# k and v of each DeltaNet head turned by VectorE in 32x32 blocks and a bounce through memory, in place of ten TensorE transposes

## What is computed

```python
qkv = silu(short_conv(qkv, conv_w)); q, k = l2norm(q), l2norm(k)
tinv = inverse(strict_lower(kb @ k.T * decay) + eye)   # u and w come from it
kd = k * exp(gc[-1] - gc)[:, None]
def step(s, xs):                                       # scan over chunks of tokens
    v_new = u_i - w_i @ s
    o_i = qg_i @ s + a_i @ v_new
    s = s * gl_i + kd_i.T @ v_new
```

## Time and profile before

| | before |
|---|---|
| median of 3 runs | 1302.97 us (1302.94 to 1303.77) |
| the profiled execution: time | 1302.37 us |
| the profiled execution: span | 1300.6 us |
| TensorE busy | 1284.3 us (99% of the span) |
| VectorE busy | 962.6 us (74%) |
| ScalarE busy | 701.2 us (54%) |
| mean memory traffic | 111 GB/s |

### The profile page before, as it was taken

How to read it: one execution, slowest core, us unless ns; L and a number is a source line. 1 busy time by engine, 2 the same in 40 slices (tenths; PEclk the granted TensorE clock), 3 DMA queues, 4 the chain that set the end, 5 groups by cost and what they waited for, 6 DMA issues and landing times.

```text
span 1300.6 us, 26090 instructions
## 1 busy us (share of the span) xinstructions
PE 1284.3 (99%) x9814; PEld 1212.4 (93%) x9814; DVE 962.6 (74%) x2396; ACT 701.2 (54%) x1578; POOL 172.8 (13%) x161
## 2 busy tenths in 40 slices
PE   7999999999999999999999999999999999999998
PEld 6898999999999999999988889999999999999998
DVE  6677867667686867767456666668999698987995
ACT  5564746465564746465366664347564355634643
POOL 1002020202001020200302320000103300041022
PEclk9999999999999999999999999999999999999999
DMA  9743543434243334325335216431323323233313
GB/s 313 242 131 96 166 122 100 118 94 118 55 142 90 116 103 120 89 72 153 115 113 169 77 51 207 124 82 33 98 67 97 98 70 93 66 100 96 83 57 106
DMA packets 207715, 144.51 MB, mean 111 GB/s; under 512 B 9455, under 2 KB 197015, under 8 KB 207463
## 3 DMA queue, kind: packets, MB, share of 16 engines
q1 hardware_dynamic: 207303, 142.72, 37.4%
q10 hardware_dynamic: 288, 0.13, 0.0%
HBM read 126.67 MB, written 17.99 MB: 111 GB/s over the span
## 4 chain that ended last, share of the span: by engine, by line
PE 92%; DVE 3%; SPq 2%; ACT 1%; issue 1%; DMA 1%; DVEq 0%; ACTq 0%
PE ps L1311 32%; PE ps L1957 25%; PE ps L1700 7%; PE ps L1615 3%; PE ps L1841 2%; PE ps L1937 2%; PE ps L1553 2%; PE ps L1622 2%; SPq L931 2%; PE ps L1439 1%; PE ps L1634 1%; PE ps L1809 1%; PE ps L1285 1%; PE ps L1795 1%; PE ps L1916 1%; PE ps L1693 1%
## 5 line engine op out<-in xcount | busy, mean ns | idle before, releaser
L1311 PE MATMUL ps<-hT_r,WAH_r 128*128 128x320 f32 x624 | 154.9, 329 | 0.5
L1311 PE MATMUL ps<-xT_r,WAH_r 128*128 128x320 f32 x624 | 142.0, 309 | 0.0
L1957 PE MATMUL ps<-d_part_r,W_r 128*128 128x320 f32 x660 | 136.7, 310 | 1.1 <-DVE xT L3388 0.7
L1311 PE MATMUL ps<-hT_r,W_r 128*128 128x320 f32 x588 | 132.6, 308 | 0.0
L1311 PEld LDWEIGHTS ps<-hT_r,WAH_r 128*128 128x128 f32 x624 | 100.3, 189 | 10.8 <-issue 9.8
L1957 PEld LDWEIGHTS ps<-d_part_r,W_r 128*128 128x128 f32 x660 | 107.5, 188 | 2.0 <-DVE xT L3388 1.3
L1957 PE MATMUL ps<-t_big_r,W_r 128*128 128x320 f32 x380 | 107.6, 311 | 0.7 <-ACT naT L2576 0.4
L1311 PEld LDWEIGHTS ps<-xT_r,WAH_r 128*128 128x128 f32 x624 | 104.5, 188 | 0.0
L1957 PE MATMUL ps<-b_part,W_r 128*128 128x320 f32 x456 | 101.2, 309 | 0.0
L1311 PEld LDWEIGHTS ps<-hT_r,W_r 128*128 128x128 f32 x588 | 97.9, 188 | 0.1
L1957 PE MATMUL ps<-t_small_r,W_r 128*128 128x320 f32 x304 | 93.9, 309 | 0.0
(11 more groups left out here) (489 smaller groups left out, 3426.7 us busy)
## 6 DMA issues: line engine op xcount, KB each, us to landing
oT<-in_ffn_w SPq DMA_DIRECT2D x44, 512.0 KB, 5.2
W<-in_w_in SPq DMA_DIRECT2D x36, 512.0 KB, 4.5
WAH<-in_w_ada SPq DMA_DIRECT2D x16, 1024.0 KB, 7.1
naT<-in_w_in SPq DMA_DIRECT2D x24, 512.0 KB, 4.2
ext_dram<-naT SPq DMA_DIRECT2D x28, 320.0 KB, 4.2
oT<-in_ffn_w SPq DMA_DIRECT2D x32, 256.0 KB, 3.9
tA<-ext_dram SPq DMA_DIRECT2D x16, 320.0 KB, 3.7
GCB<-gc_dram SPq DMA_DIRECT2D x7, 640.0 KB, 4.6
```

The lines of the kernel that those rows point to most:

```text
L1311: m = e.matmul(ps[:, bank + b, 0:n], w[:, k, :], x[:, k, a:a + n], start=k == 0 and i == 0, stop=k == KD - 1 and i == 2, skip_group_check= ...
L1957: m = e.matmul(ps[:, bank, 0:HT], w[i][:, k, :], x[i][:, k, :], start=start and k == 0 and j == 0, stop=k == half - 1 and j == 2, skip_gro ...
```

## The change

TensorE's ten transposes go. Behind "XT3" VectorE turns `kq` (k) and `conv` (v) in 32x32 blocks into the two halves of `ob`, which the scan needs only later. SyncE stores each half to memory in four transfers, behind `strip_in("k")`, waits until all eight have landed, and loads k and v back, each in one transfer, as `kT` and `vrow`, token rows with the features in quarters of 32. ScalarE makes `kd` from `kT` behind `big("4")`, ahead of its copy for P5, and VectorE makes the scaled v rows in place behind "XT diag". Both wait for both loads. The scan reads `vrow` through a view `by_quarter`. Two semaphores get new names and shared counts.

```diff
+            def turns(h):
+                for w in range(2):
+                    e.wait_ge(dve_dn.sem, dve_dn.value(h, f"{'kv'[w]} turned"))
+                    for a in range(4):
+                        e.dma_start(kv_dram[w][a, :, :, :].rearrange("j q x -> q j x"), turned[w][:, a * (TOK // 4):(a + 1) * (TOK // 4)]).then_inc(st_mid, 16)
+                e.wait_ge(st_mid, 32 + 128 * (h + 1))
+                for w in range(2):
+                    e.dma_start((kT, vrow)[w][:, :], kv_dram[w][:, :, :, :].rearrange("a j q x -> (a j) (q x)")).then_inc(ld_mid, 16)
...
                 ada_second(h)
                 if strips_after_next:
                     strip_in("k", h + 2)
+                turns(h)
                 extra_in(h, 2)
                 extra_store(h, 1)
...
             ada_second(last)
+            turns(last)
             last_strip(2)
...
-                        wait(act_dn, "kd")
-                        wait(dve_dn, "v ctx")
+                        if part == "first":
+                            e.wait_ge(raw["q"], 2)
+                        else:
+                            e.wait_ge(e_out, h * NE + 1)
...
-                filler(fill, 2)
-                if part == "first":
-                    e.wait_ge(raw["q"], 2)
-                else:
-                    e.wait_ge(e_out, h * NE + 1)
-                wait(act_dn, "silu v", h - 1)
-                for w in range(2):
-                    for t in range(NT):
-                        at = 1 + t * P + (t == CT)
-                        src = kq[:, t, 0, :] if w == 0 else conv[:, 2, at:at + P]
-                        dst = ps[:, 2 + w, t * P:(t + 1) * P] if t < CT else ps[:, 4, w * P:(w + 1) * P]
-                        m = e.transpose(dst, src, IDN)
-                pe_dn.done(m, "turn k v")
-                filler(fill, KD - 2)
+                filler(fill, KD)
...
-                wait(pe_dn, "turn k v")
-                wait(dve_dn, "v ctx")
-                for u in range(U):
-                    t = u % NT
-                    src = ps[:, 2, t * P:(t + 1) * P] if t < CT else ps[:, 4, 0:P]
-                    m = e.activation(kd[:, u, :], src, ACT.Copy, scale=prm[:, EK, u:u + 1])
-                act_dn.done(m, "kd")
...
                 big("4")
+                e.wait_ge(ld_mid, 16 * 7 + 32 * h + 32)
+                for u in range(U):
+                    m = e.activation(kd[:, u, :].rearrange("p (q c) -> p q c", q=4), by_quarter[0][:, :, u % NT, :], ACT.Copy, scale=prm[:, EK, u:u + 1])
+                act_dn.done(m, "kd")
                 wide_out("P5", "P5 wide")
...
-                vb = nrm[:, 0, 0:CT].unsqueeze(2).to_broadcast([P, CT, P])
-                done(e.tensor_tensor(vrow[:, 0:CT, :], ps[:, 3, :].rearrange("p (t c) -> p t c", t=CT), vb, ALU.mult), "v rows")
-                done(e.tensor_scalar(vrow[:, CT, :], ps[:, 4, P:2 * P], nrm[:, 0, CT:CT + 1], None, ALU.mult), "v ctx")
...
                 turn_x(3)
+                wait(act_dn, "silu v", h - 1)
+                to_k, to_v = (t.rearrange("p (a t c) -> p t a c", a=4, t=NT) for t in turned)
+                done(e.transpose(to_k, kq[:, :, 0, :].rearrange("p t (a c) -> p t a c", a=4)), "k turned")
+                e.transpose(to_v[:, 0:CT, :, :], conv[:, 2, 1:1 + LAT].rearrange("p (t a c) -> p t a c", t=CT, a=4))
+                done(e.transpose(to_v[:, CT, :, :], conv[:, 2, 2 + LAT:2 + TOK].rearrange("p (a c) -> p a c", a=4)), "v turned")
                 wait(pe_dn, "P4")
...
                 done(m, "XT diag")
+                e.wait_ge(ld_mid, 16 * 7 + 32 * h + 32)
+                vb = nrm[:, 0, :].unsqueeze(1).unsqueeze(3).to_broadcast([P, 4, NT, P // 4])
+                done(e.tensor_tensor(by_quarter[1], by_quarter[1], vb, ALU.mult), "v rows")
                 wait(act_dn, "Y5")
```

More of the change, by code:

```diff
@@ L114, in pe_steps @@
 def pe_steps():
-    names = ["turn k v"]
+    names = []
     for n in (4, 5):
@@ L127, in act_steps @@
 def act_steps():
-    names = ["kq", "L32", "L diag", "hi 1", "hi 2", "L pairs", "kd", "hi 2 late", "P4", "hi 3", "ada half", "Y4", "hi 4", "P5 wide", "P5", "Y5 wide", "Y5", "ada rows", "hi 5", "P6", "hi z", "decay", "Y6"]
+    names = ["kq", "L32", "L diag", "hi 1", "hi 2", "L pairs", "hi 2 late", "P4", "hi 3", "ada half", "Y4", "hi 4", "kd", "P5 wide", "P5", "Y5 wide", "Y5", "ada rows", "hi 5", "P6", "hi z", "decay", "Y6"]
     for s in range(NT):
@@ L164, in dve_steps @@
 def dve_steps():
-    names = ["L", "L32", "X one", "L32 turned", "L own", "L16", "L16 turned"] + [f"row {t}" for t in range(15)] + ["lo 1", "v rows", "v ctx"]
+    names = ["L", "L32", "X one", "L32 turned", "L own", "L16", "L16 turned"] + [f"row {t}" for t in range(15)] + ["lo 1"]
     for t in range(15):
         names += [f"term {t}", f"lane {t}"] + {6: ["lo 2"], 9: ["lo 2 late"]}.get(t, [])
-    names += ["X3", "XT3", "P4", "lo 3", "X4", "XT4", "lo 4"]
-    names += ["X64", "XT diag", "Y5", "XT64", "lo 5", "P6", "lo z", "Y6", "taps"]
+    names += ["X3", "XT3", "k turned", "v turned", "P4", "lo 3", "X4", "XT4", "lo 4"]
+    names += ["X64", "XT diag", "v rows", "Y5", "XT64", "lo 5", "P6", "lo z", "Y6", "taps"]
     for s in range(NT):
@@ L507, in build @@
         gain_done = sem("gain_done")
-        ld_ba = sem("ld_ba")
+        ld_mid = sem("ld_mid")
         ld_wba = sem("ld_wba")
@@ L517, in build @@
         gc_out = sem("gc_out")
-        st_gc = sem("st_gc")
+        st_mid = sem("st_mid")
         ld_gc = sem("ld_gc")
@@ L532, in build @@
         gc_dram = nc.dram_tensor("gc_dram", (2 * H, TOK), F32)
+        kv_dram = [nc.dram_tensor(f"{w}_dram", (4, P // 4, 4, TOK // 4), F32) for w in "kv"]
         x_dram = nc.dram_tensor("x_dram", (P, KD, TOK), F32)
@@ L653, in build @@
         sqkq = sb("sqkq", [P, NT, 2, P], dn)
-        sb("under_vrow", [P, 2 * 136 * U - 120 * U], dn)
+        kT = sb("kT", [P, TOK], dn)
+        sb("under_vrow", [P, 2 * 136 * U - 120 * U - TOK], dn)
         all_rows = sb("all_rows", [P, 120 * U], dn)[:, :]
-        vrow = sb("vrow", [P, NT, P], dn)
+        vrow = sb("vrow", [P, TOK], dn)
+        by_quarter = [t.rearrange("p (q t c) -> p q t c", q=4, t=NT) for t in (kT[:, :], vrow[:, :])]
         kd = sb("kd", [P, U, P], dn)
@@ L664, in build @@
         ob = sb("ob", [P, 2, NT, P], dn)
+        turned = [ob[:, w, :, :].rearrange("p t c -> p (t c)") for w in range(2)]
         prm = sb("prm", [P, NPRM, U], dn)
@@ L1030, in _ @@
             for d in range(2):
-                e.dma_start(gc_dram[d * H:(d + 1) * H, :], gcr[32 * d:32 * d + H, :]).then_inc(st_gc, 16)
-            e.wait_ge(st_gc, 32)
+                e.dma_start(gc_dram[d * H:(d + 1) * H, :], gcr[32 * d:32 * d + H, :]).then_inc(st_mid, 16)
+            e.wait_ge(st_mid, 32)
             opening(0, True)
@@ L1456, in _ @@
                     products(0)
-                    pe_dn.pass_to("turn k v")
+                    pe_dn.pass_to("P4 wide")
             def head(h, part):
@@ L1621, in head @@
                             wait(dve_dn, f"r {s} {'fb'[d]}")
-                        m = e.matmul(ps[:, (4, 6)[d], 0:P], XT[:, u, :], rr[:, d, :] if s else vrow[:, CT, :], start=True, stop=True)
+                        if s:
+                            m = e.matmul(ps[:, (4, 6)[d], 0:P], XT[:, u, :], rr[:, d, :], start=True, stop=True)
+                        else:
+                            m = e.matmul(ps[:, (4, 6)[d], 0:P].rearrange("p (q c) -> p q c", q=4), XT[:, u, :], by_quarter[1][:, :, CT, :], start=True, stop=True)
                         pe_dn.done(m, f"y {s} {'fb'[d]}")
@@ L2096, in _ @@
             round_h(7)
-            e.wait_ge(ld_ba, 16 * 7)
+            e.wait_ge(ld_mid, 16 * 7)
             e.activation(alog[:, :], alog[:, :], ACT.Exp).then_inc(ba_act, 1)
@@ L2361, in head @@
                     e.preload_act_table_set("natural_log_exp_and_others")
-                    wait(pe_dn, "turn k v")
+                    wait(dve_dn, "v turned")
                     e.wait_ge(pe_na.sem, pe_na.after("sums k 0"))
@@ L3013, in head @@
                             wait(pe_dn, f"ks {s} {'fb'[d]}")
-                            wait(dve_dn, "v ctx")
-                            done(e.scalar_tensor_tensor(rr[:, d, :], ps[:, 2 + d, 0:P], prm[:, NEG_EG, u:u + 1], vrow[:, tile[d], :], ALU.mult, ALU.add), f"r {s} {'fb'[d]}")
+                            wait(dve_dn, "v rows")
+                            r, below = (t.rearrange("p (q c) -> p q c", q=4) for t in (rr[:, d, :], ps[:, 2 + d, 0:P]))
+                            done(e.scalar_tensor_tensor(r, below, prm[:, NEG_EG, u:u + 1], by_quarter[1][:, :, tile[d], :], ALU.mult, ALU.add), f"r {s} {'fb'[d]}")
                     conv_next(s, 0)
```

10 lines of the change are left out of this document (5 added, 5 removed).

## The result

The changed kernel takes 1411.97 us (median of 4 runs, 1411.33 to 1412.46) against 1303.37 for the kernel before on the same chip: ratio 1.0832, 95% interval 1.0813 to 1.0851. The profiled execution took 1412.01 us with a span of 1410.1. So it is slower, as forecast, but by 109 us and not by 53, and outside the range.

A forecast was written before the change was run, and what follows sets the result against it. The prediction took TensorE as the bound everywhere; -8.2 (transposes) + 0.8 (X3) + 47.3 (stalls) + 13 (clock) = +53 us gave a forecast of 1356 us, range 1328 to 1378.

The forecast's parts named there:

- The mechanism and its place: Ahead of "turn P5": TensorE waits for ScalarE's copy, queued behind `kd`, which waits for the bounce; 6.2 us in heads 1 to 5.
- Landing of the stores: Transfer queue, head 2: eight stores issued 0.42 us apart behind the k strip, all landed at 250.1, bounds 248.9 and 252.1.
- a sign of being wrong: Stated test in the transfer queue: issue times far from 0.42 us, or loads landing before 248.3, would refute the forecast.
- Rival 3: Bounce slower: small 640-byte stores at half rate, 0.61 us an issue, 9.5 us a head, 1391 us; chance 0.09.
- sum of the stalls: TensorE ahead of "turn P5": 9.1 us in head 0, 31 in heads 1 to 5, 7.2 in heads 6 and 7; 47.3.
- A TensorE instruction taken away is worth its full pitch: TensorE is the bound everywhere, so removing ten transposes gives 1.02 us a head, 8.2 us in eight heads.
- the priced wait of 0.1 us a head: Ahead of "P4 wide": X3 comes 0.86 us sooner, TensorE 1.02, so TensorE waits 0.1 us a head, 0.8 in all.
- Rival 4: The bounce is hidden and the kernel is faster by what the transposes cost, 1295.6 us; chance 0.03.
- The clock: Behind the stalls TensorE's clock falls in heads 0 to 5, costing 2.2 us each (bounds 0 and 2.6), 13 us.
- Loads, `kd`, copy, VectorE's blocks: Per head: loads 4.4 us, `kd` 2.7, copy for P5 0.5; VectorE's block transposes 1.8, fitting idle time ahead of P4, cost nothing.
- The case with the blocks twice as long: VectorE behind XT3: P4's mask comes 1.6 us later, TensorE waits about 0.7; 5 us added to any case.
- Other transfers behind the new wait: SyncE's extra strip 2 and head 7's three loads and a store, held by the bounce: costed at nothing.

The follow-up runs named there:

- e1_quarters: Changed kernel with the eight stores of a head cut by quarters of the features (32 partitions each), not of the tokens: 1370.37 us, ratio 1.0510.
- e4_quarters_late: Changed kernel with stores cut by quarters of the features and `kd` moved behind ScalarE's copy for Y5: 1313.05 us, ratio 1.0075.
- e2_busy: Changed kernel with 100 idle identity matmuls in each head ahead of TensorE's wait for the copy for P5: 1480.72 us, ratio 1.1358.
- e3_late: Changed kernel with `kd` moved on ScalarE from ahead of the copy for P5 to behind the copy for Y5: 1363.59 us, ratio 1.0458.
- e8_later: e7_first with head 7's three earlier-feature loads behind extra strip 2's store, `kd` behind `big("5")`, v rows behind `small("z")`: 1297.25 us, ratio 0.9948.
- e5_all: e4_quarters_late with VectorE's lo 1 moved from behind row 14 to behind row 6 of its chain: 1308.83 us, ratio 1.0039.
- e7_first: e5_all with the eight stores and their wait ahead of the next k strip's load, heads 0 to 5: 1305.07 us, ratio 1.0015.

## Why the prediction was wrong, step by step

- **The mechanism and its place** were right: bounce late, `kd` waits, copy for P5 behind it, TensorE idle ahead of "turn P5".
- **Landing of the stores** is the step that failed. It stood as "250.1 ... Bounds: 248.9 ..., and 252.1 at half the rate". Measured on the same clock: 255.8, at a quarter of the rate, with 0.80 us an issue where 0.42 was taken, which the prediction had named as a sign of being wrong. I priced issue and bandwidth by transfers whose outermost dimension is 128 partitions, called the form of these stores equal, and did not ask how this one would be divided. Rival 3 came nearest, with stores at half the rate and 0.61 us an issue, but put it down to the small pieces, and ended at 1391. The landing mis-sized the term "sum of the stalls" (47.3) by 44 us: 14.5, 11.4 to 12.0 and 9.1 us in place of 9.1, 6.2 and 3.6. With that one thing mended (e1_quarters) the sum is 51.7.
- **"A TensorE instruction taken away is worth its full pitch"** failed. The rows that I should have set side by side are these, VectorE's lo 1 in the kernel before, ahead of the v rows:

```profile
226.32 1.22 DVE L2903 TENSOR_TENSOR naT_r<-naT,WH_more 128x1024 fp32r<-128x1024 f32 x1
```

  and the first matmuls of extra strip 0 in the same kernel:

```profile
227.68 0.54 PE L1311 MATMUL ps<-hT_r,WH_more 128*128 128x320 f32 x2
```

  lo 1 ends at 227.54, 0.14 us ahead of its reader. Without the transposes TensorE comes 1.0 us sooner and waits 1.2. The gain of 8.2 us is given back in full (8.4). I had compared TensorE with VectorE at X3 alone, where the priced wait of 0.1 us a head was never seen. Rival 4's 1295.6 could not have come from hiding the bounce by itself: e4_quarters_late, with it hidden in the middle heads, takes 1313.05, and still about 1304 without the 7.0 us of waits left in heads 0 and 7 and the 2.2 us that low clock costs behind the first.
- **The clock** was right in kind, and near in size: 13 us were taken. In the changed kernel the eight spells at 0.50 reach 2.9 to 6.1 us into the work behind each stall, 35.7 us by the clock's records, of which half is lost: 17.8 us, or 2.2 a head, as was taken for each (the expectation of e2_busy says 3 to 6 us, from the same records). What was missed is that heads 6 and 7 pay as well, behind stalls of 9 us and not 3.6. Of the rule of the Trainium skill (TensorE: Matmul & The Clock Gate, "HAM oscillation — how this bites in real kernels") the traces show just that: the fall comes in every head, not once. In e1_quarters head 7's stall of 3.5 us had one too, so my reading of the 4.4 us at the end of the earlier trace rows as a guide to which stalls are safe was wrong. At the start of the earlier trace rows the column of the granted clock reads 1.00; the lower level there was inferred from the pace of the matmuls alone.
- **Loads, `kd`, copy, VectorE's blocks**: 3.8, 3.0 and 0.5 us against 4.4, 2.7 and 0.5; the blocks took 0.85, 0.67 and 0.27, in VectorE's idle time ahead of P4, which kept 1.3 us. The case with the blocks twice as long did not arise; its price was wrong by its own rows, 242.94 + 1.6 against 244.10, which is 0.4 us a head and not 0.7.
- **Other transfers behind the new wait** were costed at nothing. In the changed kernel the stall covered them. When it went, head 7's late store showed: 7.8, 2.1, 3.2 and 2.5 us in four kernels, and nothing once it was put ahead of the loads.

The ledger of the span, 1300.6 to 1410.1: -8.2 transposes, +91.1 stalls, +8.4 lo 1, +17.8 clock, +1.7 for one more spell of 3.4 us at 0.50 ahead of head 0, +0.5 for a later first load. That is 111 against 109.5. The spell ahead of head 0 stands behind no pause of TensorE; the profiles of e1_quarters, e3_late and e8_later have it too and the others do not, so it can't be put down to the change, and its cause stays open.

## What to carry to other kernels

Before a bounce through memory is priced by bytes, look at the outermost dimension of each transfer: here 4 in place of 32 cost a factor of 2.4 in rate and 42 us. When work is taken from the bound engine, look at every place in the next stretch where it meets another engine, since what was taken may be the cover of the next wait; the list of waits does not show how thick a cover is, only the two engines' rows side by side do, as 227.54 and 227.68 above. And a result that is needed late should be made late: with the wait on a bounce in front of a copy that the bound engine needs at once, each microsecond of the bounce was paid in full, and with it as late as in e8_later next to nothing was (0.9 us, in head 0).

## What the runs showed of the hardware

- Stores of 80 KB in 128 pieces of 640 bytes passed at 85 GB/s with the DMA engines 29% busy when their targets counted (4, 32, 160), at 207 GB/s and 80% as (32, 4, 160), and at 191 GB/s and 62% as (128, 160). An issue took 0.59 (k) and 0.89 us (v) in the median in the first case, and 0.44 to 0.48 in the others.
- Pauses far shorter than those of the changed kernel were followed by a spell at half the clock: 3.5 us in head 7 of e1_quarters (spell of 3.4 us), 4.9 us in head 0 of e4_quarters_late (6.8 us), 3.2 us in head 7 of e5_all (3.4 us). The shortest was 2.25 us, in head 6 of e3_late (3.4 us); one of 2.5 us in head 7 of e7_first had none behind it.
- A matmul of 128x128 in float32 is two instructions in the trace of e2_busy, 0.112 us apart, so 0.224 us; a transpose of the same shape is one, and the ten of the kernel before started 0.11 us apart.
